# The even mixer's preparation moved into the even input projection, its output tiles in another order

## The reference, cut to what matters

```python
proj = hx @ w_in_even                                  # 31 tiles of 128 features
q, k, v = split(silu(conv4(pa[:n_qkv])))               # 12 tiles, causal convolution of width 4
q = l2n(q) * DK_A ** -0.5 ;  k = l2n(k)                # norms over each head of 128 features
g = -exp(a_log) * softplus(a_in + dt_bias)             # a_in, b_in: 4 narrow rows each
beta = sigmoid(b_in) ;  z = silu(z)                    # z: 4 tiles
r, kb, vb, w_lr, a_lr, g_lr = split(cur + (prev - cur) * mu_b)   # 14 tiles
decay = exp(-exp(-softplus(-(w0 + tanh(w_lr) @ w_w2)) - 0.5))    # low rank 64
a = sigmoid(a0 + a_lr @ w_a2)                                    # low rank 64
gb = sigmoid(g_lr) @ w_g2
kk = l2n(kb * k_k)                                     # norms over heads of 64 features
kb = kb * (1 + (a - 1) * k_a)
# the recurrences take q, k, v, cumulated g, beta, r, cumulated log decay, kb, vb, -kk, kk * a
```

## Time and profile before

| | us |
|---|---|
| median of 3 runs | 2771.08 (2759.89 to 2771.09) |
| the profiled execution | 2765.73 |
| its span | 2764.0 |
| `prepare_even` and the gaps around it (end of TensorE in the projection to the first work of `even_prompt`) | 80.3 |
| TensorE busy | 2622.5 (95% of the span) |
| VectorE busy | 1649.3 (60%) |
| ScalarE busy | 1033.1 (37%) |

### The profile page before, as it was taken

How to read it: one execution, slowest core, us unless ns; L and a number is a source line. 1 busy time by engine, 2 the same in 40 slices (tenths; PEclk the granted TensorE clock), 3 DMA queues, 4 the chain that set the end, 5 groups by cost and what they waited for, 6 DMA issues and landing times. The chain is left out here.

```text
span 2764.0 us, 52350 instructions
## 1 busy us (share of the span) xinstructions
PE 2622.5 (95%) x22668; PEld 2453.7 (89%) x22668; DVE 1649.3 (60%) x2338; ACT 1033.1 (37%) x1512; POOL 656.1 (24%) x490
## 2 busy tenths in 40 slices
PE   6999999999689998999999999999999998999998
PEld 4999988899378876999998999998989878999997
DVE  4778626742466645677862577862553256777824
ACT  4444414222533321444441444441432334444523
POOL 0456101000011021245510135510100212256301
PEclk9999999999679987999999999999999889999999
DMA  6332455621100013323245422245562114223324
GB/s 229 114 116 92 167 179 184 236 77 40 60 2 3 3 57 126 115 69 99 94 156 189 137 77 92 92 162 185 171 244 87 48 32 134 77 92 100 93 80 132
DMA packets 81053, 307.11 MB, mean 111 GB/s; under 512 B 9128, under 2 KB 14264, under 8 KB 79416
## 3 DMA queue, kind: packets, MB, share of 16 engines
q1 hardware_dynamic: 80824, 303.76, 33.0%
HBM read 292.99 MB, written 10.74 MB: 110 GB/s over the span
## 5 line engine op out<-in xcount | busy, mean ns | idle before, releaser
L174 DVE TENSOR_TENSOR weights_r<-work,weights_r 128x1024 fp32r<-128x1024 f32 (+1 forms) x332 | 424.3, 1278 | 394.3 <-ACT weights_r L170 393.4
L170 ACT ACTIVATE weights_r<-work 128x1024 fp32r<-128x1024 f32 (+1 forms) x332 | 325.6, 981 | 590.5 <-PE banks L1171 349.5
L1056 POOL TENSOR_TENSOR rows<-rows,consts 128x288 f32<-128x288 f32 (+3 forms) x64 | 88.7, 1385 | 750.5 <-ACT consts L1292 750.5
L1167 PE MATMUL banks<-low_r,weights_r 128*128 128x288 f32 (+2 forms) x912 | 234.7, 304 | 25.7 <-DVE weights_r L174 16.7
L1169 PE MATMUL banks<-low_r,weights_r 128*128 128x288 f32 (+1 forms) x1008 | 243.0, 299 | 0.0
L1169 PE MATMUL banks<-big_r,weights_r 128*128 128x288 f32 (+2 forms) x960 | 239.7, 297 | 0.0
L1171 PE MATMUL banks<-low_r,weights_r 128*128 128x288 f32 (+2 forms) x912 | 228.2, 297 | 0.0
L1074 PE MATMUL banks<-big_r,weights_r 128*128 128x288 f32 x768 | 227.1, 296 | 0.0
L1075 PE MATMUL banks<-h_r,weights_r 128*128 128x288 f32 x768 | 226.8, 295 | 0.0
L1073 PE MATMUL banks<-h_r,weights_r 128*128 128x288 f32 x768 | 226.6, 295 | 0.0
L1167 PE MATMUL banks<-h_r,weights_r 128*128 128x288 f32 (+1 forms) x832 | 204.1, 305 | 8.6 <-DVE big_r L436 8.6
(11 more groups left out here) (557 smaller groups left out, 6958.7 us busy)
## 6 DMA issues: line engine op xcount, KB each, us to landing
work<-w_ff_dram SPq DMA_DIRECT2D x118, 512.0 KB, 3.7
h<-w_mod_dram SPq DMA_DIRECT2D x48, 768.0 KB, 5.3
work<-w_down_dram SPq DMA_DIRECT2D x66, 512.0 KB, 3.6
consts<-w_ff_dram SPq DMA_DIRECT2D x58, 512.0 KB, 3.7
work<-w_mod_first_dram SPq DMA_DIRECT2D x24, 512.0 KB, 12.2
work<-w_in_even_dram SPq DMA_DIRECT2D x24, 512.0 KB, 3.9
big_buf<-w_mod_dram SPq DMA_DIRECT2D x16, 768.0 KB, 5.6
work<-w_mod_dram SPq DMA_DIRECT2D x16, 768.0 KB, 5.4
```

Of the source, the lines that this page charges most:

```text
L170: return act.activation(high, raw, ACT.Copy)
L174: return engine.tensor_tensor(low, raw, high.bitcast(F32), ALU.subtract)
L1056: pool.tensor_tensor(k.rows[:, c], k.rows[:, c], k.square[:, c], ALU.add).then_inc(added, 1)
L1167: pe.matmul(out[a], low[:, w], x[a][0], start=begins, stop=False)
```

## The change

The projection takes its tiles in the order 16 to 19, 24, 30, 0 to 7, 12 to 15, 20 to 23, 8 to 11, 25, 26 to 29. A new class `EvenGates` holds the work that was in `prepare_even`, cut into steps that the engines do in fixed iterations of the projection: `even_at(n)` is iteration n of the stage. TensorE does the four decay products after pieces 18 to 21, the sums of squares after 22 to 24, eight spreads (q and k) after 25 to 32, and the transposes after 33. SiLU, tanh and sigmoid follow each tile two iterations after its last piece; z is emptied from the banks with SiLU. The masks that the sums and spreads need, and the reset rows, are made by GpSimd. `x_kept` is stored at iteration 20's load, the constants are loaded at the end of the chain. What needs the rate `a` and the spread of kk stays behind in a short phase, `finish_even`. The core of the diff:

```diff
+EVEN_NARROW = 30
+EVEN_ROW = [16, 17, 18, 19, 24, EVEN_NARROW, *range(8), 12, 13, 14, 15, *range(20, 24), *range(8, 12), 25, *range(26, 30)]
+EVEN_STAGED = [m for m in EVEN_ROW if m < 26]
...
+    def rank(self, pe, i):
+        k = self.k
+        if i == 0:
+            pe.wait_ge(self.loaded, 16)
+            pe.wait_ge(self.mod.finished, self.mod.all)
+            pe.wait_ge(self.finished_tiles, self.finished_count(LR_B))
+        else:
+            pe.wait_ge(*self.q.after("act", f"sig_w{i - 1}"))
+        for a in range(2):
+            at = LR_B * T + a * HALF
+            last = pe.matmul(k.psum_pair(3)[:, a, 0:HALF], self.w2[0:64, i], k.big_buf[0:64, at:at + HALF],
+                             start=True, stop=True)
+        last.then_inc(*self.q.did("pe", f"w{i}"))
...
+    def sums(self, pe, g):
+        k = self.k
+        if g == 0:
+            pe.wait_ge(self.shaped, 7)
+            pe.wait_ge(*self.q.after("act", "sig_w3"))
+        pe.wait_ge(*self.q.after("act", f"squares{g}"))
+        of_kk = g == 2
+        if of_kk:
+            pe.wait_ge(*self.q.after("act", "root0"))
+        per_tile = 2 if of_kk else 1
+        for i in range(4):
+            j = i if of_kk else 4 * g + i
+            at = 32 - per_tile * (j + 1)
+            for a in range(2):
+                last = pe.matmul(k.psum_pair(3)[0:8, a, 0:HALF], self.packs[of_kk][:, at:at + 8],
+                                 self.part(i)[:, a * HALF:(a + 1) * HALF], start=j == 0, stop=j == (3 if of_kk else 7))
+        last.then_inc(*self.q.did("pe", f"sums{g}"))
+    def spread(self, pe, i):
+        if i == 0:
+            pe.wait_ge(*self.q.after("act", "root1"))
+            pe.wait_ge(*self.q.after("dve", "inverse0"))
+        else:
+            pe.wait_ge(*self.q.after("dve", f"unit{i - 1}"))
+        for a in range(2):
+            last = pe.matmul(self.k.psum_pair(3)[:, a, 0:HALF], spreads_of_qk(self.k)[:, i],
+                             self.roots[0][:, a * HALF:(a + 1) * HALF], start=True, stop=True)
+        last.then_inc(*self.q.did("pe", f"spread{i}"))
...
+    def finish_tile(self, act, tile, tile_done, count):
+        function = {LR_B: ACT.Tanh, G_B: ACT.Sigmoid}.get(tile, ACT.Silu if tile < Z_A else None)
+        if function is None:
+            return
+        at = slice(0, 64) if tile == LR_B else slice(0, P)
+        act.wait_ge(tile_done, count)
+        act.activation(self.big(tile)[at], self.big(tile)[at], function).then_inc(self.finished_tiles, 1)
...
+    def squares(self, act, g):
+        if g == 0:
+            act.wait_ge(self.mod.finished, self.mod.all)
+        else:
+            act.wait_ge(*self.q.after("pe", f"sums{g - 1}"))
+        act.wait_ge(self.finished_tiles, self.finished_count(K_A + 3))
+        for i in range(4):
+            scale = 1.0 if g < 2 else self.k.par("k_k")[:, i:i + 1]
+            last = act.activation(self.part(i), self.big((Q_A, K_A, K_B)[g] + i), ACT.Square, scale=scale)
+        last.then_inc(*self.q.did("act", f"squares{g}"))
+    def root(self, act, of_kk):
+        act.wait_ge(*self.q.after("pe", f"sums{1 + of_kk}"))
+        act.activation(self.roots[of_kk].rearrange("p (a t) -> p a t", a=2), two_halves(self.k.psum_pair(3), HALF)[0:8],
+                       ACT.Sqrt, bias=self.k.eps[0:8, 0:1]).then_inc(*self.q.did("act", f"root{of_kk}"))
+    def soft(self, act):
+        did, after = self.q.did, self.q.after
+        rows, dt_bias = self.k.rows, self.k.par("dt_bias")
+        act.wait_ge(*after("dve", "rows_b"))
+        act.activation(self.softp, rows[0:4, :], ACT.Abs, bias=dt_bias[0:4, :]).then_inc(*did("act", "abs"))
+        act.wait_ge(*after("act", "abs"))
+        act.activation(self.softp, self.softp, ACT.Exp, scale=-1.0).then_inc(*did("act", "exp"))
+        act.wait_ge(*after("act", "exp"))
+        act.activation(self.softp, self.softp, ACT.Ln, bias=1.0).then_inc(*did("act", "ln"))
+        act.activation(self.rate, self.k.par("a_log")[0:4, :], ACT.Exp).then_inc(*did("act", "exp_a_log"))
+        act.wait_ge(*after("dve", "rows_clear"))
+        act.activation(rows[32:36, :], self.rows_b, ACT.Sigmoid).then_inc(*did("act", "beta"))
...
+    def unit(self, dve, i):
+        x = self.big(Q_A + i).rearrange("p (a t) -> p a t", a=2)
+        dve.wait_ge(*self.q.after("pe", f"spread{i}"))
+        dve.scalar_tensor_tensor(out=x, in0=x, scalar=128.0 ** -0.5 if i < 4 else 1.0, in1=two_halves(self.k.psum_pair(3), HALF),
+                                 op0=ALU.mult, op1=ALU.mult).then_inc(*self.q.did("dve", f"unit{i}"))
+    def narrow(self, dve, staged_count):
+        did, after, rows = self.q.did, self.q.after, self.k.rows
+        dve.wait_ge(*staged_count)
+        dve.wait_ge(*after("dve", "inverse1"))
+        dve.tensor_copy(self.rows_b, rows[32:36, :]).then_inc(*did("dve", "rows_b"))
+        dve.wait_ge(*after("dve", "rows_b"))
+        dve.memset(rows[32:64, :], 0.0)
+        dve.memset(rows[64:128, :], 0.0).then_inc(*did("dve", "rows_clear"))
+        dve.wait_ge(*after("act", "abs"))
+        dve.tensor_scalar(rows[0:4, :], rows[0:4, :], self.k.par("dt_bias")[0:4, :], 0.0, ALU.add, ALU.max)\
+            .then_inc(*did("dve", "relu"))
+    def cumulated(self, dve):
+        did, after, rows, softp = self.q.did, self.q.after, self.k.rows, self.softp
+        dve.wait_ge(*after("act", "exp_a_log"))
+        dve.wait_ge(*after("dve", "relu"))
+        dve.tensor_tensor(softp, rows[0:4, :], softp, ALU.add).then_inc(*did("dve", "softplus"))
+        dve.wait_ge(*after("dve", "softplus"))
+        dve.tensor_scalar(softp, softp, self.rate, -1.0, ALU.mult, ALU.mult).then_inc(*did("dve", "g"))
+        dve.wait_ge(*after("dve", "g"))
+        dve.tensor_tensor_scan(rows[0:4, :], self.resets[0:4, :], softp, 0.0, ALU.mult, ALU.add).then_inc(*did("dve", "gc"))
...
+                    for norm in even_norms:
+                        if i == even_at(0):
+                            sp.dma_start(k.xbuf_in, k.io["xbuf_in"].rearrange("p k s t -> p (k s t)"))\
+                                .then_inc(norm.xbuf_loaded, 16)
+                        if i == even_at(12):
+                            sp.wait_ge(norm.last_rows, 2)
+                            sp.dma_start(k.io["xbuf_s_out"].rearrange("p k s t -> p (k s t)"), k.xbuf_out)\
+                                .then_inc(norm.xbuf_stored, 16)
+                            sp.dma_start(k.io["xbuf_p_out"], k.last_rows).then_inc(norm.xbuf_stored, 16)
+                            even_gates.load(sp)
+                        if i == even_at(20):
+                            sp.dma_start(k.x_kept, k.x).then_inc(norm.x_kept, 16)
+                for norm in even_norms:
...
+                        if even_gates and i in range(even_at(18), even_at(22)):
+                            even_gates.rank(pe, i - even_at(18))
+                        if even_gates and i in range(even_at(22), even_at(25)):
+                            even_gates.sums(pe, i - even_at(22))
+                        if even_gates and i in range(even_at(25), even_at(33)):
+                            even_gates.spread(pe, i - even_at(25))
+                        if even_gates and i == even_at(33):
+                            even_gates.columns(pe)
...
+                    if even_gates:
+                        v = ends.get(i - 2)
+                        if v and v.kind == "proj_even" and 1 in v.sides and v.m < 26:
+                            place = EVEN_STAGED.index(v.m)
+                            even_gates.finish_tile(act, even_tile(v.m), tile_done, place + 1)
+                        if i in range(even_at(19), even_at(23)):
+                            even_gates.decay_rates(act, i - even_at(19))
+                        if i == even_at(21):
+                            even_gates.squares(act, 0)
+                        if i == even_at(23):
+                            even_gates.squares(act, 1)
+                        if i == even_at(24):
+                            even_gates.root(act, 0)
+                            even_gates.squares(act, 2)
+                        if i == even_at(25):
+                            even_gates.root(act, 1)
+                        if i == even_at(29):
+                            even_gates.soft(act)
+                        if i == even_at(31):
+                            even_gates.to_end(act)
+                        if i == even_at(34):
+                            even_gates.column_copies(act)
...
+                    if even_gates:
+                        if i in range(even_at(19), even_at(23)):
+                            even_gates.decay_sums(dve, i - even_at(19))
+                        if i in (even_at(24), even_at(25)):
+                            even_gates.inverse(dve, i - even_at(24))
+                        if i in range(even_at(26), even_at(34)):
+                            even_gates.unit(dve, i - even_at(26))
+                        if i == even_at(29):
```

(78 more changed lines are left out.)

380 lines of the change are left out of this document (159 added, 221 removed).

## The result

The changed kernel takes 2756.24 us (median of 6 runs, 2744.33 to 2758.66); the kernel before, on the same chip, 2769.47 (6 runs, 2759.89 to 2774.49). The ratio is 0.9941, 95% interval 0.9922 to 0.9960: 13 us faster, where the sum had 29.4, the forecast was 2738 and the range ended at 2753. The profiled executions took 2755.76 and 2765.73.

What follows compares the result with a forecast made beforehand. The projection was taken as TensorE-bound, the phase behind it as a chain of dependent steps. Sum: -80.3 + 15.5 + 24.3 + 9.1 + 2 = -29.4, giving 2736.3 (profiled) or 2741.7 (median); forecast 2738, range 2720 to 2753.

Steps and rivals of the forecast that it cites:

- The phase goes, 80.3: The phase between the projection's last product and `even_prompt`, a chain of dependent steps, disappears: 80.3 us off.
- The small products inside the projection, 24.3: TensorE in the projection: 96 added records at 0.24 us, 23.3, plus 1.0 for transposes; 24.3 us on.
- The short rest, 15.5: `finish_even` with its gaps: 2.2 + 12.5 + 0.75 = 15.5 us on, ends 14 and 21.
- Iterations 29 and 30, 9.1: Late projection: TensorE waits 7.75 us, then 1.35, for VectorE products queued behind ScalarE's chain; 9.1 us on.
- the clock in it, 2: After that stall, products run at half clock for a time: 0 to 2.7 us, taken as 2.
- The second wait: Late projection: after spread 5 and piece 31, TensorE waits 1.35 us for VectorE's next product.
- ScalarE and VectorE elsewhere, transfers, order of tiles, nothing: Rest of the projection: added ScalarE and VectorE work fits, transfers have cover, the new tile order costs nothing; 0 us.
- rival B: Projection: TensorE finds each step unready, twelve waits of 1 to 1.5 us; gain 11 to 17, about 2753; chance 0.12.
- rival A: Iterations 29 and 30: no stall, so the 9.1 + 2 go; gain 40, 2727 us; chance 0.12.
- C: Projection's second half: the clock falls to 0.50 and stays, making the kernel slower, 2879 us; chance 0.02.

Runs made afterwards that it cites:

- Experiment 1: The changed kernel with 128-row operands, zero weights in the added rows, for spreads and rate products; 2742.18 us, ratio 0.9889.
- experiment 2: The changed kernel with the rest's products in two groups, four spreads and then four rate products; 2753.34 us, ratio 0.9926.
- experiment 6: The changed kernel with 128-row operands for the spreads alone, rate products left at 64 rows; 2751.68 us, ratio 0.9941.
- experiment 5: The changed kernel with 128-row spreads and rate products and the softplus chain spread over four iterations, the rest's order unchanged; 2735.28 us, ratio 0.9879.
- 7: The changed kernel with 128-row operands, split softplus chain and spreads grouped before rate products, timed again beside experiment 5; 2731.38 us, ratio 0.9873.
- 4: The changed kernel with 128-row operands, spreads grouped before rate products, and the softplus chain spread over four iterations; 2736.42 us, ratio 0.9867.

## Why the prediction was wrong

*The phase goes, 80.3:* right (80.2 if the last product's end is added up from the earlier trace rows, 688.03). Nothing of it came back that isn't in the terms below.

*The small products inside the projection, 24.3:* mis-sized. They cost 4 x 1.35 + 3 x 4.17 + 8 x 1.35 + 1.0 = 29.7 us, 5.4 more. The price per record was taken from records of one kind in a row; here each group of decays or spreads stands between products of 128 rows, and pays about 0.19 on entry and again on exit. The mechanism (no idle time, each record counts, full clock) was right. Experiment 1 takes the excess out for the spreads. A rule of the Trainium skill ("TensorEngine Tiling (Array Packing)", "Key Properties") bears on this: a change of tiling mode, not of the tile alone, drains TensorE. It gives no figure; by experiments 1, 2 and 6 the traces agree that a change costs time, for operands of 8, 64 and 128 rows, with 0.19 us at full clock and 0.28 at half. The sums have 128 rows and an excess of 0.33 per 16 records, so rows don't explain it. A change in the number of columns (8 against 128) was not tried, but the changed kernel's trace speaks for it: its transposes have 128 rows throughout, and their single records start 0.11 us apart while they have 128 columns, 0.20 apart where 128 columns give way to 64.

*The short rest, 15.5:* the step that failed most. It took 22.7 us, 7.2 more and above the end of 21 that I had put to it. The gaps at its ends were right (2.3 and 0.7). The term that failed is the 12.5 between, chosen on the word that "the clock is up at the start": it was 0.50 from 732, half a microsecond after the first product, and 7 changes of rows came on top, so TensorE's chain set the end. Between the gaps 19.8 us were measured. TensorE's 32 records took 17.3 of them, where 32 x 0.48 = 15.4 and 7 x 0.28 = 2.0 for the changes make 17.4. The last sigmoid and the VectorE operations behind it took 2.5. The prediction's own figure for half clock throughout was 17.7 (16.0 and 1.7); it had the records a little too dear, its tail too short, and no change of rows at all. I had the row that shows small products losing the clock behind dense ones, and took a mean of both ends of it instead of asking what would bring the clock back. Experiment 1 shows what would: operands of 128 rows.

*Iterations 29 and 30, 9.1, and the clock in it, 2:* right in place, cause and size (10.1 against 11.1). The second wait did not come, since TensorE was slow at half clock just then. It began spread 6 at 698.98, and VectorE's product was ready at 696.90; at full clock TensorE would have come 3.0 sooner, at about 696.0, and waited 0.9. So the 3.0 and the 1.35 are in part the same time. The Trainium skill's rule on a drain behind a table load ("ScalarE: Activation LUTs", "What ACT_TABLE_LOAD costs") was rightly turned down: Abs to beta, with four loads in it, took 8.3 us again.

*ScalarE and VectorE elsewhere, transfers, order of tiles, nothing:* right; TensorE has no other wait there. With this rival B falls (it named waits of 1 to 1.5 us before each step), rival A falls with the 7.1 us wait, and C with a clock of 1.00 from 560 to 684 and from 695 to the end of the projection.

The terms as measured: -80.3 + 22.7 + 29.7 + 10.1 = -17.8, and `even_prompt` starts 17.6 us earlier, counted from the projection's start. The sum was thus 11.6 too hopeful: 7.2 in the rest, 5.4 in the small products, less 1.0 in the stall. A gain of 17.8 would still have put the time at about 2753, the range's end, from the 2771.08 the prediction started from.

Of the 17.6 us, 9.9 are left at the end of the profiled execution and 13 in the medians. The prediction has no term for the code behind `even_prompt`, which is the same in all nine kernels. Yet it took 1995.8 us before and 2002.1 after; in the others 1990.2 (experiment 5), 2000.1, 2002.3, 2003.0, 2005.5, 2005.8 and 2007.0. The clock accounts for most of that. In this part TensorE was busy at half clock for 124.6 us before, 133.1 after and 111.6 in experiment 5; taking half of each kernel's figure off its time leaves 1932.9 to 1938.7 in all nine. One place shows it, the kernel before first and the changed one second (windows):

```profile
1026.90:1054.20 27.30, 27.30 (x274) 24.26 (x274) 8.33 (x13) 2.34 (x5) 7.51 (x4) 0.50 0.01 2
1008.50:1042.60 34.10, 34.10 (x306) 30.88 (x306) 9.38 (x14) 2.35 (x5) 7.52 (x4) 0.50 0.01 1
```

The stretch is 34.1 us long in the changed kernel and in all experiments but the fifth, where it is 13.6. Executions of one kernel differ in the same way: of 17 of the kernel before, timed beside experiments 5 to 7, the fastest (2757.97) had a mean clock of 0.962, the slowest (2781.68) of 0.952. Whether the change makes the clock behind `even_prompt` lower, or it falls as it falls, one profile of each kernel does not settle; the time of before lies inside the others' spread.

## What to carry to other kernels

Price a small matrix product by the shape of what stands in front of and behind it, not by records in a row: here each change of the number of rows cost TensorE 0.19 us at full clock and 0.28 at half, and where TensorE had little but products of 8 and 64 rows to do, the clock stayed at 0.50 once it had fallen, which doubled the price of each record. Where the operand's missing rows can be had as zeros in the weights, the product with all 128 rows was no dearer (0.24 us a record), lost the change, and the clock came back. A chain of dependent short steps with table loads belongs, cut into one or two steps at a time, into the idle time of many iterations; put whole into one, it delays what is queued behind it on the same engine.

## What the runs showed of the hardware that was not expected

A change between products of 128, 64 and 8 rows cost 0.19 us at full clock (1.35 against 0.96 for a group between dense products, two changes) and 0.28 at half (2.21 against 1.93, one change). The granted clock stayed at 0.50 through 13 us of gapless products of 8 and 64 rows (experiment 2), and through 128 and 64 rows by turns (experiment 6), and rose from 0.50 to 1.00 in the midst of them when all had 128 (experiment 1, at 732.8). With 128 rows everywhere it still fell at the start of the rest in three kernels of four, for 3.4 us each (experiment 1 at 729.3, 4 at 718.9, 7 at 717.8), and in experiment 5 it did not. What made it fall there is open. Each of these rests on one profile of its kernel.
